# Gated projection in tall pieces: 1024 rows by 128 columns instead of 512 by 256

## The chip, the cores and the metric

The kernel runs on one core of a Trainium2 chip. The metric is the device time of one execution in microseconds. Before the change it is 2535.25 us, the median of three runs (2534.98 to 2535.69).

## The reference, cut to what matters

A decoder trunk of two layers over 256 positions of width 2048. Layer 0 mixes with gated DeltaNet heads and RG-LRU channels, layer 1 with sliding-window attention; each layer then cross-attends and applies a gated MLP. The change touches only the first product of layer 0, the combined input projection:

```python
h = rmsnorm(x, norm_mix[l])
if l % 2 == 0:
    qkv, z, b_raw, a_raw, lx, lg = split_cols(h @ hyb_in_w[e], HYB_SIZES)
    oa = gdn_mixer(qkv, z, b_raw, a_raw, ...)      # conv of width 4 and silu on q, k, v; chunked delta rule; gate z
    ob = rglru_mixer(lx, lg, ...)                  # conv of width 4, recurrence, gate lg
```

All is float32. `h @ hyb_in_w` is 256 x 2048 by 2048 x 6160 columns, of which the 16 for the gates are computed apart.

## The kernel before, in words

**Products in two parts.** Weights stream from HBM in pieces of 128x1024 values (512 KB), each as NK = 4 blocks of 128 rows by COLS = 256 columns. ScalarE rounds a piece to the matmul format (`w_hi`, L581), VectorE takes the rest (`w_lo`, L1048). The activations `h` are held as hi and low parts as well, side by side: `h[:, kt, 0]` and `h[:, kt, 1]`, 256 positions each. A product is hi x hi + hi x low + low x hi, three matmuls of 256 columns (L1754 to L1756). A group is 256 output columns: four pieces, 16 blocks of rows. Its result is one PSUM bank of 128 x 512: the two tiles of 128 channels, 256 positions each. Groups alternate between the banks ST[0] and ST[1]. A "wide" piece (L1759 to L1773), used elsewhere in the kernel, streams both parts of `h` in one matmul of 512 columns into two banks and leaves two halves that are added later.

**Order.** The hybrid stage has four pairs of heads, p = 0 to 3, each of 24 ticks, t = 0 to 23. One tick is one piece; six groups a pair, j = 0 to 5: q, k, v, z, the LRU's input, the LRU's gate (gi = 6p + j). On each engine the order is written out by hand. TensorE runs piece t (it waits for `lo_split` of that piece, and at the group's first piece for `group_evac` of the group two before), then the small products of `hyb_front(p, t)` for this pair and `hyb_tail(p - 1, t)` for the one before. ScalarE and VectorE run the split for piece t + 3 (AHEAD = 3) and then their own parts of front and tail; at t = 10 and 14 VectorE runs its front ahead of the split.

**Evacuation.** VectorE multiplies a finished bank by `rstd` (evac_scaled, L1053 to L1058): at t = 3, 7, 15, 19 and 23 right after the group's last piece, and for v (j = 2) only at t = 13, behind four mask products (L1266 to L1269) that wait for TensorE's products of tick 13 (`lx_done`). Destinations are the conv pads for q, k, v and the LRU input, `z_silu` for z and `k_buf` (as `gl_`) for the gate. The convs follow (L1100, L1103, L1111), then silu on ScalarE. Other steps that the prediction names: the squares and logs of q and k on ScalarE (L697 to L705), VectorE's output of the pair before (L1363, L1364), q and k normed (L1253, L1254), TensorE's grams (L1885), the mask products of levels (L1286), TensorE's chunk products (L1877, L1899), v_new (L1338), its use (L1982 to L1990), the state update (L1225), the scans (L1354), the LRU's decay (L1318).

**Loads.** SyncE issues a load (L447) as soon as `lo_split` has freed the raw buffer, four buffers in turn.

Of the kernel before, what the change touches and what calls it, by code (L numbers as in the profile page):

```python
# [26 lines left out]
ALU = mybir.AluOpType  # L27
# [3 lines left out]
P = 128  # L31
TOK = 256
# [21 lines left out]
COLS = 256  # L54
NRAW = 4
NSPLIT = 4
# [39 lines left out]
N_MEM = [0, 4]  # L96
N_XQ = [2, 16]
N_ROPE = 6


def mix_order(layer, t):
# [79 lines left out]
def trunk(nc, a, out):  # L181
    ctx = ExitStack()
    with ctx:
        def sb(name, shape, dt=F32, scope=ctx):
            return scope.enter_context(nc.sbuf_tensor(name, shape, dt))
# [50 lines left out]
        with s1:  # L236
            pads = sb("conv_pads", [P, 2, 2, TOK + 3], scope=s1)
            qb = sb("q_buf", [P, 512], scope=s1)
            kb = sb("k_buf", [P, 512], scope=s1)
            vbuf = sb("v_buf", [P, 512], scope=s1)  # L240
            zs = sb("z_silu", [P, 512], scope=s1)
            W4 = sb("gdn_work", [P, 4, 512], scope=s1)
            kbe = sb("k_beta_exp", [P, 512], scope=s1)
            kdec = sb("k_dec", [P, 512], scope=s1)
            vb = sb("v_beta", [P, 512], scope=s1)
            LT = sb("LT", [P, 512], scope=s1)
            Ufull = sb("U_blocks", [P, 512], scope=s1)
            qd = sb("q_dec", [P, 512], scope=s1)
            usb = sb("u", [P, 512], scope=s1)
            wsb = sb("wT", [P, 512], scope=s1)  # L250
            vnew = sb("v_new", [P, P], scope=s1)
            St = sb("state", [P, 256], scope=s1)
            egl = sb("exp_gl", [P, 8], scope=s1)
            ro = sb("o_rstd", [P, 512], scope=s1)
            xc = sb("lru_x", [P, 512], scope=s1)
            rt = sb("lru_r", [P, 512], scope=s1)
            it = sb("lru_i", [P, 512], scope=s1)
            l2 = sb("lru_l2", [P, 512], scope=s1)

            l1, gl_, osq = vbuf[:], kb[:], usb[:]  # L260
            msq = [qb[:], W4[:, 3, :]]
            ba_rows = usb[0:16, 0:TOK]
            x_ss, x_total, x_log, x_err = lp[:, 0, 0:8], lp[:, 1, 0:2], lp[:, 1, 2:4], lp[:, 1, 4:6]
# [81 lines left out]
        w_loaded = [sem(f"w_loaded{i}") for i in range(NRAW)]  # L345
        hi_split, lo_split = sem("hi_split"), sem("lo_split")
        pieces_done, group_evac = sem("pieces_done"), sem("group_evac")
        dve_link, act_link = sem("dve_link"), sem("act_link")
        x_loaded = [sem(f"x_loaded{i}") for i in range(4)]
        ident_loaded, c_loaded, p_loaded, b_loaded = sem("ident_loaded"), sem("c_loaded"), sem("p_loaded"), sem("b_loaded")  # L350
# [87 lines left out]
        @block.sync  # L438
        def _(sp):
            xv_ = a["x"].rearrange("b (t p) d -> p (b t) d", p=P)  # L440
            sp.dma_start(cst[:, 0:2 * P], a["consts"][:, 0:2 * P]).then_inc(ident_loaded, 16)

            def load(n, k, turn, src, rows, c0):

                if not isinstance(n, int) or n >= NRAW:
                    sp.wait_ge(lo_split, n - NRAW + 1)
                sp.dma_start(raw[:, k], src[rows:rows + NK * P, bass.ds(c0, COLS)]  # L447
                             .rearrange("(k p) c -> p k c", p=P)).then_inc(w_loaded[k], 16)

            def load_group(n, src, c0, quarters=4):  # L450
                for q in range(quarters):
                    if n == HYB:
                        sp.dma_start(x_tok[:, :, 512 * q:512 * q + 512], xv_[:, :, 512 * q:512 * q + 512]).then_inc(x_loaded[q], 16)
                    load(n + q, (n + q) % NRAW, 0, src, q * NK * P, c0)
                if n == HYB:
                    sp.dma_start(cst[:, 2 * P:], a["consts"][:, 2 * P:]).then_inc(c_loaded, 16)

            hyb = a["hyb_in_w"][0]
            starts = [0, 1024, 2048, 3072, 4112, 5136]
            for p in range(PAIRS):  # L460
                for j, s in enumerate(starts):
                    load_group(HYB + p * PAIR_TICKS + 4 * j, hyb, s + p * COLS)

            def load_mem(layer):
                for g in range(4):
                    load_group(MEM[layer] + 4 * g, a["xkv_w"][layer], g * COLS)

            def load_common(layer, mixout):
                for t in range(32):
                    g, q = mix_order(layer, t)  # L470
                    load(MIXOUT[layer] + t, t % NRAW, 0, mixout, q * NK * P, g * COLS)
                for g in range(2):
                    load_group(XQ[layer] + 4 * g, a["xq_w"][layer], g * COLS)
                if layer == 0:
                    load_mem(1)
                for g in range(8):
                    load(XO[layer] + g, g % NRAW, 0, a["xo_w"][layer], 0, g * COLS)
                for c, size, tile, n, g in ffn_parts(layer):
                    with sp.Fori(0, size // 2) as i:
                        for half in range(2):  # L480
                            for q in range(4):
                                load(n + 4 * half + q + i * 8, q, 0, a["ffn_in_w"][layer], q * NK * P,
                                     half * F_FF + tile * P + i * COLS)
                    n += 4 * size
                    quarters = size // 4
                    for g in range(8):
                        for q in range(quarters):
                            load(n + g * quarters + q, (g * quarters + q) % NRAW, 0, a["ffn_out_w"][layer],
                                 (tile + 4 * q) * P, g * COLS)

            load_mem(0)
            load_common(0, a["hyb_out_w"][0])
            for g in range(4):
                load_group(SWKV + 4 * g, a["swa_in_w"][0], SWA_HEADS * SWA_HD + g * COLS)
            for g in range(8):
                load_group(SWQ + 4 * g, a["swa_in_w"][0], g * COLS)
            load_common(1, a["swa_out_w"][0])
            for s in o_stored:
                sp.wait_ge(s, 16 * 4)
# [538 lines left out]
        def _(dve):  # L1038
# [14 lines left out]
            def evac_scaled(dst, start, gi, n, i=0, rows=rstd):  # L1053
# [3 lines left out]
                bank = B[4] if gi in (GROUP[XQ[0]], GROUP[SWKV]) else ST[gi % 2]  # L1057
                v.tensor_tensor(dst, two(bank[:]), r, ALU.mult).then_inc(group_evac, 1)  # L1058

            def refine(r, u, total, width):  # L1060

                link(v.scalar_tensor_tensor(u, total, EPS * width, r, ALU.add, ALU.mult))
                link(v.scalar_tensor_tensor(u, u, -0.5 / width, r, ALU.mult, ALU.mult))
                return v.scalar_tensor_tensor(r, u, 1.5, r, ALU.add, ALU.mult)
# [164 lines left out]
            def hyb_front(p, t):  # L1229
# [40 lines left out]
                if t in (3, 7, 13):  # L1270
                    if t == 13:
                        j, gi, n = 2, gi - 1, n - 2
                    if p:
                        if j < 2:
                            dve.wait_ge(lt_ready, p)
                        else:
                            dve.wait_ge(vT_done, p)
                    evac_scaled(pads[:, gi % 2, :, 3:3 + TOK], HYB, gi, n)
                    dve.wait_ge(group_evac, gi + 1)
                    if t == 3 and p:  # L1280
                        state_update(p - 1, 3)
                    qkv_conv(p, j, (0,) if t == 13 else (0, 1))
# [6 lines left out]
                if t == 19:  # L1289
                    if p:  # L1290
                        dve.wait_ge(lru_out, p)
                    evac_scaled(pads[:, gi % 2, :, 3:3 + TOK], HYB, gi, n)
                if t >= 15 and t % 2:
                    dve.wait_ge(tu_done, 5 * p + level)
                    dve.wait_ge(tu_ready, 6 * p + level)
# [8 lines left out]
                if t == 15:  # L1304
                    if p:
                        dve.wait_ge(gdn_out, p)
                    evac_scaled(two(zs[:]), HYB, gi, n)
                if t == 19:
                    pad = pads[:, gi % 2]
                    dve.wait_ge(group_evac, gi + 1)  # L1310
# [7 lines left out]
                        last = v.tensor_scalar(rt[:, s], rt[:, s], 1.0, lruc[:, 2, 2 * p + b:2 * p + b + 1], ALU.add, ALU.mult)  # L1318
                    last.then_inc(la_ready, 1)
                if t == 23:  # L1320
                    evac_scaled(two(gl_), HYB, gi, n)

            def hyb_tail(p, t):
                if t == 0:
# [56 lines left out]
            for p in range(PAIRS):  # L1381
                for t in range(PAIR_TICKS):
# [16 lines left out]
                    if p:  # L1399
                        hyb_tail(p - 1, t)  # L1400
                    elif t not in (6, 10, 11):
                        gates(t)
                    if p == 1 and t == 0:
                        kq = lambda name: par[:, PCOL[name]:PCOL[name] + DEPTH]
                        link(v.tensor_tensor(key_gain, kq("xq_norm"), kq("xk_norm"), ALU.mult))
# [323 lines left out]
        def _(pe):  # L1729
# [8 lines left out]
            def piece(n, gi, q, last_q, src, kts, bank=None, between=None):  # L1738
# [17 lines left out]
                        last = mm(o, wlo[:, k, kk, w], src[:, kt, 0, :], start=False, stop=final, skip_group_check=True)  # L1756
                last.then_inc(pieces_done, 1)

            def wide_piece(n, gi, q, kts, i, src=h, last_q=3):  # L1759

                k = n % NSPLIT
# [268 lines left out]
            for p in range(PAIRS):  # L2030
                for t in range(PAIR_TICKS):
                    if p == 0 and t < 4:
                        h_is("x")(t)
                    piece(HYB + PAIR_TICKS * p + t, 6 * p + t // 4, t % 4, 3, h, range(4 * (t % 4), 4 * (t % 4) + 4))
                    hyb_front(p, t)
                    if p:
                        hyb_tail(p - 1, t)
# [368 lines left out]
```

## Time and profile before

| | |
|---|---|
| median of three runs | 2535.25 us |
| profiled execution | 2536.81 us |
| its span | 2535.0 us |
| granted TensorE clock | 0.999 |
| TensorE, VectorE, ScalarE busy | 99%, 69%, 45% |
| hybrid stage | pieces 0 to 95, up to about 409 us |

The times in the rows further down are microseconds from the start of the span. A matmul's length in a row includes its way through the array, so rows of consecutive matmuls overlap: the distance of their starts is what one costs.

### The profile page before, as it was taken

How to read it: one execution, taken by the hardware profiler on the slowest of the kernel's cores; microseconds unless marked ns; L12 is line 12 of the kernel's file. 1: busy time of each engine (PE TensorE's matmuls, PEld its weight loads, DVE VectorE, ACT ScalarE, POOL GpSimd, SP SyncE). 2: the span in 40 equal slices, each digit the busy share in tenths (PEclk: the TensorE clock that was granted, in tenths of full speed). 3: DMA queues.
4: the chain of work that ended last, by engine and by line, in shares of the span. 5: the costliest groups of instructions: out<-in, count | busy, mean ns of one | idle time of the engine just before them, and what ended most of it. 6: DMA issues, size and time to landing. Idle time of an engine off the chain costs nothing.

```text
span 2535.0 us, 44491 instructions
## 1 busy us (share of the span) xinstructions
PE 2510.7 (99%) x17345; PEld 2257.2 (89%) x17345; DVE 1757.0 (69%) x2483; ACT 1143.6 (45%) x1532; POOL 50.1 (2%) x58
## 2 busy tenths in 40 slices
PE   8999999999999999999999999999999999999999
PEld 7999998989988888888888999998888888888888
DVE  6676676677777657775678767776777667765774
ACT  6444455445444434443444445544444334433443
POOL 2000000010000000000000000010000000000000
PEclk9999999999999999999999999999999999999999
DMA  7444444554565655665565543353555655655654
GB/s 221 126 142 125 134 133 135 180 188 157 158 190 183 193 188 178 195 193 188 183 191 182 177 138 114 125 175 125 172 179 187 199 188 184 192 191 176 197 191 149
DMA packets 428439, 432.34 MB, mean 171 GB/s; under 512 B 13802, under 2 KB 425747, under 8 KB 428304
## 3 DMA queue, kind: packets, MB, share of 16 engines
q1 hardware_dynamic: 423776, 422.46, 52.9%
q0 software_dynamic: 2304, 5.85, 0.8%
q8 instruction: 99, 1.62, 0.3%
q10 hardware_dynamic: 2224, 2.11, 0.3%
q14 instruction: 36, 0.29, 0.0%
HBM read 428.27 MB, written 2.10 MB: 170 GB/s over the span
## 4 chain that ended last, share of the span: by engine, by line
PE 94%; DVE 3%; ACT 2%; issue 1%; DMA 0%; SPq 0%; ACTq 0%; DVEq 0%
PE stream L1769 41%; PE stream L1772 20%; PE stream L1754 8%; PE stream L1755 8%; PE stream L1756 8%; PE bank L1877 1%; PE bank L1736 1%; DVE w_lo L1048 1%; ACT w_hi L581 1%; DVE k_buf L1111 0%; PE bank L2322 0%; PE bank L1945 0%; PE bank L1804 0%; PE bank L2296 0%; PE bank L2303 0%
## 5 line engine op out<-in xcount | busy, mean ns | idle before, releaser
L1048 DVE TENSOR_TENSOR w_lo<-w_raw,w_hi 128x1024 fp32r<-128x1024 f32 x800 | 963.3, 1222 | 476.7 <-ACT w_hi L581 473.9
L581 ACT CAST w_hi<-w_raw 128x1024 fp32r<-128x1024 f32 x800 | 835.9, 1049 | 748.9 <-PE stream L1772 628.7
L1769 PE MATMUL stream<-h,w_hi 128*128 128x512 f32 x2816 | 884.7, 395 | 0.0
L1772 PEld LDWEIGHTS stream<-h,w_lo 128*128 128x128 f32 x2816 | 529.0, 188 | 125.1
L1772 PE MATMUL stream<-h,w_lo 128*128 128x256 f32 x2816 | 553.2, 278 | 0.0
L1769 PE MATMUL stream<-act,w_hi 128*128 128x512 f32 x1664 | 523.3, 396 | 0.0
L1754 PE MATMUL stream<-h,w_hi 128*128 128x256 f32 x1536 | 455.2, 296 | 2.2 <-DVE w_lo L1048 2.2
L1755 PE MATMUL stream<-h,w_hi 128*128 128x256 f32 x1536 | 435.2, 283 | 0.0
L1756 PE MATMUL stream<-h,w_lo 128*128 128x256 f32 x1536 | 435.1, 283 | 0.0
L1769 PEld LDWEIGHTS stream<-h,w_hi 128*128 128x128 f32 x2816 | 428.8, 189 | 0.1
L1772 PEld LDWEIGHTS stream<-act,w_lo 128*128 128x128 f32 x1664 | 312.6, 188 | 73.9
L1772 PE MATMUL stream<-act,w_lo 128*128 128x256 f32 x1664 | 327.0, 278 | 0.0
L1754 PEld LDWEIGHTS stream<-h,w_hi 128*128 128x128 f32 x1536 | 294.6, 192 | 16.3 <-issue 11.3
L1755 PEld LDWEIGHTS stream<-h,w_hi 128*128 128x128 f32 x1536 | 295.0, 192 | 4.0 <-issue 3.6
L1756 PEld LDWEIGHTS stream<-h,w_lo 128*128 128x128 f32 x1536 | 294.8, 192 | 0.0
L1769 PEld LDWEIGHTS stream<-act,w_hi 128*128 128x128 f32 x1664 | 253.4, 189 | 0.0
L1482 DVE TENSOR_TENSOR ffn_cross<-stream,ffn_cross 128x512 f32<-128x512 f32 x88 | 60.9, 692 | 96.3 <-ACT ffn_cross L930 96.3
L930 ACT COPY ffn_cross<-stream 128x512 f32<-128x512 f32 x88 | 51.7, 587 | 152.5 <-PE stream L1772 152.5
L1754 PE MATMUL stream<-act,w_hi 128*128 128x256 f32 x336 | 97.8, 291 | 0.0
L1755 PE MATMUL stream<-act,w_hi 128*128 128x256 f32 x336 | 95.1, 283 | 0.0
L1756 PE MATMUL stream<-act,w_lo 128*128 128x256 f32 x336 | 95.1, 283 | 0.0
L1111 DVE SCALAR_TENSOR_TENSOR ffn_conv<-ffn_pad,par,ffn_conv 128x256 f32<-128x256 f32 x176 | 77.5, 482 | 13.1 <-DVE ffn_conv L1103 6.7
(425 smaller groups left out, 1887.9 us busy)
## 6 DMA issues: line engine op xcount, KB each, us to landing
w_raw<-in_ffn_in_w SPq DMA_DIRECT2D x352, 512.0 KB, 4.4
w_raw<-in_ffn_out_w SPq DMA_DIRECT2D x176, 512.0 KB, 3.4
w_raw<-in_hyb_in_w SPq DMA_DIRECT2D x96, 512.0 KB, 3.8
w_raw<-in_swa_in_w SPq DMA_DIRECT2D x48, 512.0 KB, 3.5
w_raw<-in_xkv_w SPq DMA_DIRECT2D x32, 512.0 KB, 3.4
w_raw<-in_hyb_out_w SPq DMA_DIRECT2D x32, 512.0 KB, 4.4
w_raw<-in_swa_out_w SPq DMA_DIRECT2D x32, 512.0 KB, 3.6
w_raw<-in_xq_w SPq DMA_DIRECT2D x16, 512.0 KB, 4.1
```

Source lines behind the costliest of these rows:

```text
L581: nc.scalar.copy(whi[:, k], raw[:, n % NRAW]).then_inc(hi_split, 1)
L930: nc.scalar.copy(two(frt[:, t // 4]), wide(g0 + t // 4)[:, :, TOK:512]).then_inc(ffn_right, 1)
L1048: v.tensor_tensor(wlo[:, k], raw[:, n % NRAW], whi[:, k].bitcast(F32), ALU.subtract).then_inc(lo_split, 1)
L1111: last = v.scalar_tensor_tensor(d, tap, par[:, col(j, b)], d, ALU.mult, ALU.add)
L1482: v.tensor_tensor(two(frt[:, t // 4]), both[:, :, 0:TOK], two(frt[:, t // 4]), ALU.add).then_inc(group_evac, 1)
L1736: return nc.tensor.transpose(o, i, ident)
L1754: mm(o, whi[:, k, kk, w], src[:, kt, 0, :], start=first, stop=False, skip_group_check=True)
L1755: mm(o, whi[:, k, kk, w], src[:, kt, 1, :], start=False, stop=False, skip_group_check=True)
L1756: last = mm(o, wlo[:, k, kk, w], src[:, kt, 0, :], start=False, stop=final, skip_group_check=True)
L1769: mm(bank[:, m, :], whi[:, k, kk, w], src[:, kt, :, :], start=(q == 0 and kk == 0), stop=False, skip_group_check=True)
L1772: last = mm(bank[:, m, 0:TOK], wlo[:, k, kk, w], src[:, kt, 0, :], start=False, stop=(q == last_q and kk == len(kts) - 1), skip_group_chec ...
L1877: last = mm(bank[rows, o + u * CHUNK:o + u * CHUNK + CHUNK], lhs[rows, s], rhs[rows, s], start=True, stop=True)
```

## The change

For 22 of the 24 groups (all but the first and the last) a piece has another shape: 1024 rows by 128 columns. A group's pieces 0 and 1 are then the first tile of 128 channels over all 2048 rows, and pieces 2 and 3 the second tile. The raw, hi and low buffers are the same memory, read as 8 blocks of 128 rows and 128 columns. Each block is one matmul of 512 columns (hi weights with hi and low parts of `h`) and one of 256 (low weights with the hi part), into one bank per tile: the first tile has ST[1], the second ST[0]. VectorE multiplies the bank by `rstd` into `tile_parts` and adds its two halves into the destination. The first tile is evacuated at the end of VectorE's ticks t = 2, 6, 10, 14, 18, 22, the second where the whole group was. TensorE waits at a group's first piece for `first_tile_evac` of the group before, and at its third for `group_evac` of the group before.

```diff
+TALL = range(1, 6 * PAIRS - 1)
+def tall(slot):
+    return slot.rearrange("p a (b c) -> p (a b) c", c=P)
...
+            def load_tall(n, src, c0):
+                for i in range(4):
+                    m, half = i // 2, i % 2
+                    if n + i >= NRAW:
+                        sp.wait_ge(lo_split, n + i - NRAW + 1)
+                    sp.dma_start(tall(raw[:, (n + i) % NRAW]),
+                                 src[half * 8 * P:half * 8 * P + 8 * P, c0 + m * P:c0 + m * P + P]
+                                 .rearrange("(k p) c -> p k c", p=P)).then_inc(w_loaded[(n + i) % NRAW], 16)
...
+            def evac_tile(dst, gi, m, n):
+                dve.wait_ge(pieces_done, n + 1)
+                dve.wait_ge(first_tile_evac if m else group_evac, gi)
+                bank = ST[1 - m]
+                link(v.tensor_tensor(two(parts[:]), two(bank), rstd[:].unsqueeze(1).to_broadcast([P, 2, TOK]), ALU.mult))
+                v.tensor_tensor(dst, parts[:, 0:TOK], parts[:, TOK:512], ALU.add).then_inc(group_evac if m else first_tile_evac, 1)
+            def evac_hyb(p, j, n, tiles):
+                gi = 6 * p + j
+                pad = pads[:, gi % 2]
+                for m in tiles:
+                    flat = slice(m * TOK, m * TOK + TOK)
+                    evac_tile(zs[:, flat] if j == 3 else gl_[:, flat] if j == 5 else pad[:, m, 3:3 + TOK], gi, m, n)
...
-                    evac_scaled(pads[:, gi % 2, :, 3:3 + TOK], HYB, gi, n)
+                    if gi in TALL:
+                        evac_hyb(p, j, n, (1,))
+                    else:
+                        evac_scaled(pads[:, gi % 2, :, 3:3 + TOK], HYB, gi, n)
...
+                    if t % 4 == 2 and 6 * p + t // 4 in TALL:
+                        if t == 14 and p:
+                            dve.wait_ge(gdn_out, p)
+                        evac_hyb(p, t // 4, HYB + PAIR_TICKS * p + t - 1, (0,))
...
+            def tall_piece(n, gi, t):
+                k, m, half = n % NSPLIT, t // 2, t % 2
+                pe.wait_ge(lo_split, n + 1)
+                if half == 0 and m == 0 and gi > 1:
+                    pe.wait_ge(first_tile_evac, gi - 1)
+                if half == 0 and m == 1:
+                    pe.wait_ge(group_evac, gi)
+                bank, hi, lo = ST[1 - m], tall(whi[:, k]), tall(wlo[:, k])
+                for kk in range(0, 8, 2):
+                    for e in (kk, kk + 1):
+                        mm(bank, hi[:, e, :], h[:, 8 * half + e, :, :], start=(half == 0 and e == 0), stop=False, skip_group_check=True)
+                    for e in (kk, kk + 1):
+                        last = mm(bank[:, 0:TOK], lo[:, e, :], h[:, 8 * half + e, 0, :], start=False,
+                                  stop=(half == 1 and e == 7), skip_group_check=True)
+                last.then_inc(pieces_done, 1)
...
-                    piece(HYB + PAIR_TICKS * p + t, 6 * p + t // 4, t % 4, 3, h, range(4 * (t % 4), 4 * (t % 4) + 4))
+                    if 6 * p + t // 4 in TALL:
+                        tall_piece(HYB + PAIR_TICKS * p + t, 6 * p + t // 4, t % 4)
+                    else:
+                        if 6 * p + t // 4 == TALL[-1] + 1 and t % 4 == 0:
+                            pe.wait_ge(first_tile_evac, len(TALL))
+                        piece(HYB + PAIR_TICKS * p + t, 6 * p + t // 4, t % 4, 3, h, range(4 * (t % 4), 4 * (t % 4) + 4))
```

The evacuations at t = 15, 19 and 23 change in the same way as the one shown.

## Rows read from the trace of the kernel before

**Rows 1.** The page: busy time by engine, and the chain by engine.
```profile
PE 2510.7 (99%) x17345; PEld 2257.2 (89%) x17345; DVE 1757.0 (69%) x2483; ACT 1143.6 (45%) x1532; POOL 50.1 (2%) x58
...
PE 94%; DVE 3%; ACT 2%; issue 1%; DMA 0%; SPq 0%; ACTq 0%; DVEq 0%
```

**Rows 2.** Timeline of TensorE, old pieces in pair 0 (start us, length us, ...).
```profile
43.16 0.28 PE L1756 MATMUL stream<-h,w_lo 128*128 128x256 f32 x1
...
49.28 0.28 PE L1756 MATMUL stream<-h,w_lo 128*128 128x256 f32 x1
```

**Rows 3.** Timeline of TensorE, wide pieces of the FFN.
```profile
1000.25 0.39 PE L1772 MATMUL stream<-h,w_lo 128*128 128x256 f32 x2
...
1011.39 0.39 PE L1772 MATMUL stream<-h,w_lo 128*128 128x256 f32 x2
```

**Rows 4.** Timeline of TensorE and VectorE, pair 1, tick 13 and piece 14.
```profile
169.90 0.68 PE L1899 MATMUL bank<-cst,LT 64*64 64x64 f32 x16 [0.22 <-DVE q_dec L1262]
...
170.52 0.39 PE L1754 MATMUL stream<-h,w_hi 128*128 128x256 f32 x1
...
170.90 0.42 DVE L1266 TENSOR_TENSOR gdn_work<-bank,cst 128x256 f32<-128x256 f32 x1
...
172.03 0.42 DVE L1269 TENSOR_TENSOR gdn_work<-cst,gdn_work 128x256 f32<-128x256 f32 x1
...
172.37 0.68 DVE L1058 TENSOR_TENSOR conv_pads<-stream,rstd 128x512 f32<-128x512 f32 x1
```

**Rows 5.** Timeline of VectorE, pair 1, tick 14, and TensorE's piece 16.
```profile
175.03 0.42 DVE L1286 TENSOR_TENSOR gdn_work<-bank,cst 128x256 f32<-128x256 f32 x1
...
177.19 1.22 DVE L1048 TENSOR_TENSOR w_lo<-w_raw,w_hi 128x1024 fp32r<-128x1024 f32 x1
...
178.33 0.39 PE L1754 MATMUL stream<-h,w_hi 128*128 128x256 f32 x1
```

**Rows 6.** Timeline of VectorE, pair 2, ticks 2 to 4; TensorE's piece 4 and tick 5.
```profile
225.22 1.27 DVE L1354 TENSOR_TENSOR_SCAN lru_x<-lru_r,lru_i 128x256 f32<-128x256 f32 x2
226.53 1.23 DVE L1048 TENSOR_TENSOR w_lo<-w_raw,w_hi 128x1024 fp32r<-128x1024 f32 x1
...
233.33 0.28 DVE L1338 TENSOR_TENSOR v_new<-u,bank 128x128 f32<-128x128 f32 x1
...
227.17 0.39 PE L1754 MATMUL stream<-h,w_hi 128*128 128x256 f32 x1
...
233.67 0.66 PE L1990 MATMUL stream<-q_dec,state 128*128 128x64 f32 x4
```

**Rows 7.** Timeline of VectorE, pair 1, ticks 7 to 10; TensorE's grams of tick 11.
```profile
144.99 0.69 DVE L1058 TENSOR_TENSOR conv_pads<-stream,rstd 128x512 f32<-128x512 f32 x1 [1.14 <-PE stream L1756]
...
159.29 0.69 DVE L1254 TENSOR_TENSOR k_buf<-k_buf,gdn_work 128x512 f32<-128x512 f32 x1
...
160.03 0.45 PE L1885 MATMUL bank<-k_buf 128*64 128x64 f32 x8
```

**Rows 8.** Timeline of VectorE, pair 0, ticks 6 and 7.
```profile
46.71 2.36 DVE L1048 TENSOR_TENSOR w_lo<-w_raw,w_hi 128x1024 fp32r<-128x1024 f32 x2
49.24 0.69 DVE L1058 TENSOR_TENSOR conv_pads<-stream,rstd 128x512 f32<-128x512 f32 x1 [0.17 <-PE stream L1756]
```

**Rows 9.** Timeline of VectorE, pair 1, tick 22, and TensorE's next piece 0.
```profile
209.52 0.61 DVE L1318 TENSOR_SCALAR lru_r<-lru_r,lru_cols 128x256 f32<-128x256 f32 x2
...
211.28 0.39 PE L1754 MATMUL stream<-h,w_hi 128*128 128x256 f32 x1
```

**Rows 10.** Busy time from 100 to 410 us (window, us, engines, clock, DMA, GB/s).
```profile
100.00:410.00 310.00, 307.72 (x3128) 287.16 (x3127) 214.32 (x362) 154.46 (x225) 1.42 (x2) 1.00 0.44 131
```

**Rows 11.** The casts (page), queue 1 from 200:300, the gain queue from 0:8.
```profile
L581 ACT CAST w_hi<-w_raw 128x1024 fp32r<-128x1024 f32 x800 | 835.9, 1049 | 748.9 <-PE stream L1772 628.7
...
q1 hardware_dynamic: 13276, 13.19, 45.0%
...
q10 hardware_dynamic: 48, 0.02, 0.8%
```

More of the change, by code:

```diff
@@ L239, in trunk @@
             kb = sb("k_buf", [P, 512], scope=s1)
+            parts = sb("tile_parts", [P, 512], scope=s1)
             vbuf = sb("v_buf", [P, 512], scope=s1)
@@ L347, in trunk @@
         pieces_done, group_evac = sem("pieces_done"), sem("group_evac")
+        first_tile_evac = sem("first_tile_evac")
         dve_link, act_link = sem("dve_link"), sem("act_link")
@@ L461, in _ @@
                 for j, s in enumerate(starts):
-                    load_group(HYB + p * PAIR_TICKS + 4 * j, hyb, s + p * COLS)
+                    if 6 * p + j in TALL:
+                        load_tall(HYB + p * PAIR_TICKS + 4 * j, hyb, s + p * COLS)
+                    else:
+                        load_group(HYB + p * PAIR_TICKS + 4 * j, hyb, s + p * COLS)
             def load_mem(layer):
@@ L1291, in hyb_front @@
                         dve.wait_ge(lru_out, p)
-                    evac_scaled(pads[:, gi % 2, :, 3:3 + TOK], HYB, gi, n)
+                    evac_hyb(p, j, n, (1,))
                 if t >= 15 and t % 2:
@@ L1306, in hyb_front @@
                         dve.wait_ge(gdn_out, p)
-                    evac_scaled(two(zs[:]), HYB, gi, n)
+                    evac_hyb(p, j, n, (1,))
                 if t == 19:
@@ L1320, in hyb_front @@
                 if t == 23:
-                    evac_scaled(two(gl_), HYB, gi, n)
+                    if gi in TALL:
+                        evac_hyb(p, j, n, (1,))
+                    else:
+                        evac_scaled(two(gl_), HYB, gi, n)
             def hyb_tail(p, t):
@@ L2033, in _ @@
                         h_is("x")(t)
-                    piece(HYB + PAIR_TICKS * p + t, 6 * p + t // 4, t % 4, 3, h, range(4 * (t % 4), 4 * (t % 4) + 4))
+                    if 6 * p + t // 4 in TALL:
+                        tall_piece(HYB + PAIR_TICKS * p + t, 6 * p + t // 4, t % 4)
+                    else:
+                        if 6 * p + t // 4 == TALL[-1] + 1 and t % 4 == 0:
+                            pe.wait_ge(first_tile_evac, len(TALL))
+                        piece(HYB + PAIR_TICKS * p + t, 6 * p + t // 4, t % 4, 3, h, range(4 * (t % 4), 4 * (t % 4) + 4))
                     hyb_front(p, t)
```

## The prediction

> **What bounds the kernel now.** I read the page first: TensorE is busy 99% of the span and makes 94% of the chain of waits, VectorE is busy 69% [rows 1]. So every microsecond that TensorE waits is a microsecond of the run, and VectorE costs nothing until something on TensorE waits for it. Then I read the timeline of the hybrid stage engine by engine, because the change moves the points at which TensorE may wait for VectorE. I write "piece t" and "tick t" for tick t of a pair, 0 to 23; TensorE's small products of a tick stand behind its piece. TensorE waits in this stage only a few tenths at a time (0.22 us for the end of LT's group, [rows 4]), and what VectorE does in a tick is late by design: its split at tick t is for the piece of tick t+3.
>
> **The piece itself.** The old piece has 24 matmuls of 256 columns. From 43.16 to 49.28 us lie 51 of them [rows 2]: 0.120 each, 2.88 us a piece. The tall piece has 8 of 512 and 8 of 256, in the order of the wide piece that layer 0 and the FFN run: two 512, two 256. Sixteen such fours take 1011.39 - 1000.25 = 11.14 us [rows 3], 0.696 each, four to a piece: 2.785 us. Saved: 0.095 us a piece, 88 pieces, 8.4 us if nothing else moves. The columns streamed are the same (6144); only the eight fewer instructions are saved. No row shows two 512s into one bank; the old pieces' 256s all go to one bank and hold 0.120, so I bound that from 0 to 8.4 us for all and take 0.095 a piece. The Trainium skill (TensorE: Matmul & The Clock Gate, "Back-to-back issue gap") gives an isolated matmul N/2.4 + 2.5 ns, which would be 109 and 216 ns, a saving of 0.02 us a piece; the rows have 120 and a mean of 174, so the trace pays more per instruction than that rule, and by the rule the sum below would be some 2.4 us higher.
>
> **What VectorE gets.** Per group one multiply of 128x512 (0.69 [rows 4]) becomes two, each followed by a linked add of 128x256, which I price with the 0.42 of the 128x256 product of the same engine [rows 4]: 0.69 + 0.04 for the link + 0.42 = 1.15 us a tile, 2.3 a group, some 1.6 x 22 = 35 us more work. VectorE has the room on average [rows 10]. Not everywhere: the bank turns round faster. Before, a group had its bank for two groups' time; the evacuation at tick 4j+3 was needed at piece 4j+8. Now tile 1 of group j, still evacuated there, is needed by piece 4j+6, and tile 0, evacuated at the very end of VectorE's tick 4j+2, by piece 4j+4. I laid these needs over the timeline in all four pairs; the rows repeat in each to a few hundredths.
>
> **(e) Tick 13, the large one.** Group j=2 is evacuated not at tick 11 but at tick 13, behind four mask products that wait for TensorE's products of tick 13. TensorE starts piece 14 at 170.52, right behind those. VectorE starts the masks at 170.90 and the evacuation only at 172.37 [rows 4]. Piece 14 is now the first of tile 1 and waits for exactly that evacuation: 172.37 + 0.69 + 0.04 + 0.42 + 0.05 to cross = 173.57. Stall 3.05 us, in each pair: 12.2 us. It can't be hidden: the masks need TensorE's tick 13, which stands directly ahead of piece 14. Queued behind it on TensorE is everything.
>
> **(g) Tick 14.** After the evacuation VectorE has half a conv, a mask, the other half and a split, and only then tile 0 of j=3, which piece 16 needs. Before, from the mask at 175.03 to the split at 177.19 are 2.16 us, and piece 16 starts at 178.33 [rows 5]. With TensorE's products of tick 14 now ending near 177.3, mask 177.3, split 179.4 to 180.7, tile 0 until 181.7; TensorE could start piece 16 at 181.2. +0.5 us a pair.
>
> **(b) Ticks 2 to 5, pairs 1 to 3.** Tick 2 ends with two scans, and the split of tick 3 starts at 226.53; piece 4 starts at 227.17 [rows 6]. Tile 0 of j=0 goes between, with 0.3 us of delay from gelu and ScalarE's queue (the added 0.46 on the evacuation of tick 23): scans end 226.7, tile 0 227.9, piece 4 at 227.95: +0.8. Then the row of VectorE work from the split at 226.53 to v_new at 233.33 has no gap, and TensorE's product at 233.67 wants v_new, which is done at 233.61 [rows 6]. That row starts 1.3 us later and has 0.46 more in it: v_new at 235.4, the product at 235.4, +1.75 in all. By tick 7 VectorE has caught up.
>
> **(d) Ticks 7 to 11.** From the end of piece 7 there is one closed chain: evacuation 144.99, conv, silu, squares, a table load, the log and exp of o, VectorE's output of the pair before, the norm of k at 159.29, TensorE's grams at 160.03 [rows 7]. The add lengthens it by 0.46. Pieces 8 to 11 end earlier, for nothing. In pair 0 that chain has other parts: the split at 46.71 and its follower run without a gap up to the evacuation at 49.24 [rows 8], tile 0 of j=1 goes between, and conv and the gate values behind it come 1.4 later; TensorE has some 0.2 there to give, so +1.2.
>
> **(a) Piece 0 of the next pair.** The scale of lru_r ends at 210.13, tile 0 of j=5 follows until 211.3, piece 0 starts at 211.28 [rows 9]: +0.07, and the savings of pieces 22 and 23 go into it, since the chain before it runs over ScalarE.
>
> **What of the saving remains.** Where a chain over VectorE decides, shorter pieces wait. It remains for pieces 6, 7, 14 and 16 to 21 (nine in pairs 1 and 2, seven in pairs 0 and 3): 32 of 88, 3.0 us. The others had it taken by (a), (b), (d), (g) and by the chain over exp and LT before tick 13, where TensorE already waited [rows 4].
>
> **The loads.** Each row of a load is 512 bytes instead of 1024, 1024 packets instead of 512. Between 200 and 300 us queue 1 used 45.0% of 16 x 100 us for 13276 packets, 54 ns each with the tiny ones; the gain load's queue had 0.8% of 16 x 8 us for 48 packets, 32 of them of 512 bytes: at most 32 ns each [rows 11]. So a load needs 64 x 32 = 2.0 us of each DMA engine against 1.7, in a tick of 4.07 us on average (piece 16 at 178.33, piece 4 of the next pair at 227.17, twelve ticks [rows 5, 6]). ScalarE's casts wait for TensorE, not for a load [rows 11]. I take 0; bounds 0 and, were packets as dear as before (3.5 us in a tick of 4.07), some 5. The Trainium skill (DMA: Bandwidth & Descriptors, "Why small descriptors are slow") has a fixed three cycles a packet on 32-byte beats: 2 x 19 / 35, 9% more DMA time, nothing for the run either; the rows allow 17% and more.
>
> **Sum.** (e) 4 x 3.05 = 12.2. (g) 4 x 0.5 = 2.0. (b) 3 x 1.75 = 5.25, in which the saving of its pieces is already spent. (d) 3 x 0.46 + 1.2 = 2.6. (a) 3 x 0.07 = 0.2. Less 3.0. Together +19.2 us. The profiled execution took 2536.81 us (span 2535.0, 1.8 around it), so 2556.0 for it; it lies 1.6 above the median 2535.25, so 2554.5 for a median. Behind the hybrid stage TensorE is again at work without a break, so nothing of it is given back.
>
> **Rivals.**
> 1. Only the wait at piece 14 is real, the smaller ones lie within slack that I misjudge (the add is shorter, TensorE's waits take up what VectorE is late). For it: my margins in (a), (b), (g) are tenths. Against: the row of VectorE work in (b) has no gap at all. 12.2 less the saving of 80 pieces, 7.6: +4.6, 2540.
> 2. Faster: the wait isn't there, because group j=2's bank is free by piece 14, and all pieces keep their 0.095. It decides at one point: the evacuation at 172.37 would have to end before 170.5. Against it: that evacuation stands behind work that itself waits for TensorE. 2535.25 - 8.4 = 2526.9.
> 3. The lateness of VectorE feeds on itself: splits come late, ScalarE (silu, casts) behind them, and piece 6, 10 or 18 waits too. For it: VectorE is busy 214 of 310 us in the stage [rows 10], 69%, and the 35 us more make it 80%. Against it: the split that ends at 178.41 is for piece 17, which can't start before piece 16 at 178.33 has run its 2.88 [rows 5], so splits have some 3 us to give. Another 2.5 us a pair: +29, 2564.
> 4. Loads become late: another 5 on the sum, 2559.5; it needs packets as dear as double the size.
>
> **Chances.** Forecast 0.62, rival 1 0.14, rival 2 0.04, rival 3 0.14, rival 4 0.03; the rest (0.03) is that 512-column matmuls into one bank go slower. A measurement of this kernel tells 0.2% (5 us) from no change. Faster 0.04, same 0.07 (half of rival 1), slower 0.89. The range of 8 in 10 is 2543 to 2564: below it lie rival 2 and most of rival 1, above it part of rival 3.
>
> **What would show it.** (e): TensorE idle by about 3 us before one tall matmul in each pair, released by VectorE's add into conv_pads. (b): a wait of 0.8 for the add at piece 4 and about 1 for v_new. (g): 0.5 before piece 16. Piece: 0.696 per four. Loads: landing of hyb_in under 5 us, no cast that waits for one. I am wrong if piece 14 starts without a wait, or if the hybrid stage is longer by under 10 or over 28 us, or if the rest of the run changes.

## The result, and the profile after

The changed kernel takes 2564.26 us (2563.52 to 2564.79, four runs) against 2535.47 beside it: ratio 1.0114, 95% interval 1.0102 to 1.0125, 28.8 us slower. Forecast were 19.2 us and a range of 2543 to 2564. The direction and the waits held; the sum was a third short, mainly because one term was missing from it, the price of a halved clock behind each long wait, and the time lies 0.26 us outside the range.

The two profiled executions are 28.0 us apart (2564.79 and 2536.81). Piece 96, the first behind the hybrid stage, starts at 440.42 us against 412.25, 28.2 later; from there to the end both take the same (2122.6 and 2122.7 us). The prediction's own sign of being wrong, a stage longer by over 28, was thus met.

The page after, with busy time by engine, the chain by engine, and the groups of the tall piece (L1818, L1820), the old piece (L1802) and the split (L1070):

```profile
PE 2513.1 (98%) x16641; PEld 2225.4 (87%) x16641; DVE 1787.6 (70%) x2549; ACT 1143.4 (45%) x1532; POOL 50.1 (2%) x58
...
PE 88%; DVE 7%; ACT 3%; issue 2%; DMA 0%; DVEq 0%; SPq 0%; ACTq 0%
...
L1818 PE MATMUL stream<-h,w_hi 128*128 128x512 f32 x704 | 236.2, 417 | 18.0 <-DVE conv_pads L1088 15.0
L1802 PE MATMUL stream<-h,w_hi 128*128 128x256 f32 x832 | 246.1, 296 | 1.7 <-DVE w_lo L1070 1.7
L1820 PE MATMUL stream<-h,w_lo 128*128 128x256 f32 x704 | 142.1, 284 | 0.0
```

Beside [rows 1], TensorE has fallen from 94% of the chain to 88% and VectorE has risen from 3% to 7%: the chain now runs through VectorE where TensorE waits. Of the 18.0 us that TensorE sat idle before the tall matmuls of L1818, 15.0 were ended by the add into conv_pads.

The timeline of TensorE in pair 1, from the products of tick 13 to piece 15, answers to [rows 4] (start, length, then the idle time before and what ended it):

```profile
178.32 0.68 PE L1964 MATMUL bank<-cst,LT 64*64 64x64 f32 x16 [0.38 <-DVE q_dec L1300]
182.06 0.76 PE L1818 MATMUL stream<-h,w_hi 128*128 128x512 f32 x2 [3.06 <-DVE conv_pads L1088]
182.61 0.63 PE L1820 MATMUL stream<-h,w_lo 128*128 128x256 f32 x2
183.04 1.05 PE L1818 MATMUL stream<-h,w_hi 128*128 128x512 f32 x2
183.90 0.63 PE L1820 MATMUL stream<-h,w_lo 128*128 128x256 f32 x2
184.33 1.05 PE L1818 MATMUL stream<-h,w_hi 128*128 128x512 f32 x2
185.18 0.63 PE L1820 MATMUL stream<-h,w_lo 128*128 128x256 f32 x2
185.61 0.80 PE L1818 MATMUL stream<-h,w_hi 128*128 128x512 f32 x2
```

The wait for the add is there with 3.06 us, as forecast. What I had not forecast stands in the rows behind it: a four of matmuls (two of 512 columns, two of 256) takes 1.29 us (183.04 to 184.33) instead of 0.70. The same stretches by the windows view (window, its length, busy PE, PEld, DVE, ACT, POOL, granted clock, DMA share, GB/s):

```profile
76.60:83.40 6.80, 5.89 (x26) 4.92 (x28) 2.54 (x6) 0.00 (x0) 0.00 (x0) 0.51 0.23 68
83.40:182.40 99.00, 92.08 (x768) 77.42 (x766) 74.82 (x130) 47.56 (x68) 0.00 (x0) 1.00 0.49 128
182.50:185.90 3.40, 3.40 (x13) 2.96 (x12) 1.29 (x3) 0.00 (x0) 0.00 (x0) 0.51 0.05 13
186.00:284.80 98.80, 92.55 (x774) 77.74 (x772) 73.86 (x126) 47.57 (x68) 0.00 (x0) 1.00 0.48 125
284.90:288.30 3.40, 2.85 (x9) 2.51 (x10) 2.21 (x5) 0.00 (x0) 0.00 (x0) 0.51 0.36 107
288.40:387.20 98.80, 93.33 (x778) 78.39 (x777) 73.10 (x125) 47.57 (x68) 0.00 (x0) 1.00 0.47 123
387.40:394.10 6.70, 5.55 (x19) 4.60 (x20) 2.77 (x6) 0.00 (x0) 0.00 (x0) 0.50 0.22 75
```

In each pair, about when the wait at piece 14 ends, the granted clock falls to half (1.2 instead of 2.4 GHz), for 6.8, 3.4, 3.4 and 6.8 us, and is whole again until the next. Before the change it was 1.00 in all of this stage. The Trainium skill (TensorE: Matmul & The Clock Gate, "What's actually happening") says that the array's clock is gated to half when the engine has been idle and given back by activity; these rows agree in kind, each fall standing behind 3.06 or 3.07 us of idle time, and I had left that rule out of the sum.

### The profile page after: what moved, and what is told of

Its sections match the earlier page's. It is cut to its first block, busy times and chain, and to the rows that moved or that the text cites. A ratio compares the mean times of both kernels' runs of the same rounds, so it can differ in the third digit from the quotient of the medians.

```text
span 2563.0 us, 43197 instructions
## 1 busy us (share of the span) xinstructions
PE 2513.1 (98%) x16641; PEld 2225.4 (87%) x16641; DVE 1787.6 (70%) x2549; ACT 1143.4 (45%) x1532; POOL 50.1 (2%) x58
## 4 chain that ended last, share of the span: by engine, by line
PE 88%; DVE 7%; ACT 3%; issue 2%; DMA 0%; DVEq 0%; SPq 0%; ACTq 0%
PE stream L1834 41%; PE stream L1837 20%; PE stream L1802 5%; PE stream L1803 5%; PE stream L1804 5%; PE stream L1818 3%; DVE w_lo L1070 2%; PE stream L1820 1%; PE bank L1784 1%; ACT w_hi L603 1%; PE bank L1942 1%; DVE tile_parts L1087 1%; ACT L609 1%; DVE k_buf L1149 0%; DVE q_buf L1149 0%
## 5 line engine op out<-in xcount | busy, mean ns | idle before, releaser
L1070 DVE TENSOR_TENSOR w_lo<-w_raw,w_hi 128x1024 fp32r<-128x1024 f32 x800 | 963.6, 1221 | 469.0 <-ACT w_hi L603 466.4
L1834 PE MATMUL stream<-h,w_hi 128*128 128x512 f32 x2816 | 884.8, 396 | 0.0
L1837 PE MATMUL stream<-h,w_lo 128*128 128x256 f32 x2816 | 553.1, 278 | 0.0
L1834 PEld LDWEIGHTS stream<-h,w_hi 128*128 128x128 f32 x2816 | 428.8, 189 | 0.1
L1837 PE MATMUL stream<-act,w_lo 128*128 128x256 f32 x1664 | 327.0, 278 | 0.0
L1818 PE MATMUL stream<-h,w_hi 128*128 128x512 f32 x704 | 236.2, 417 | 18.0 <-DVE conv_pads L1088 15.0
L1802 PE MATMUL stream<-h,w_hi 128*128 128x256 f32 x832 | 246.1, 296 | 1.7 <-DVE w_lo L1070 1.7
L1803 PE MATMUL stream<-h,w_hi 128*128 128x256 f32 x832 | 236.0, 284 | 0.0
L1804 PE MATMUL stream<-h,w_lo 128*128 128x256 f32 x832 | 235.9, 284 | 0.0
L1802 PEld LDWEIGHTS stream<-h,w_hi 128*128 128x128 f32 x832 | 159.8, 192 | 9.0 <-issue 8.3
L1820 PEld LDWEIGHTS stream<-h,w_lo 128*128 128x128 f32 x704 | 135.8, 193 | 32.5
L1803 PEld LDWEIGHTS stream<-h,w_hi 128*128 128x128 f32 x832 | 160.0, 192 | 2.4 <-issue 2.2
L1820 PE MATMUL stream<-h,w_lo 128*128 128x256 f32 x704 | 142.1, 284 | 0.0
L1818 PEld LDWEIGHTS stream<-h,w_hi 128*128 128x128 f32 x704 | 111.2, 194 | 27.1 <-issue 23.7
```

Source lines behind the costliest of these rows:

```text
L1070: v.tensor_tensor(wlo[:, k], raw[:, n % NRAW], whi[:, k].bitcast(F32), ALU.subtract).then_inc(lo_split, 1)
L1802: mm(o, whi[:, k, kk, w], src[:, kt, 0, :], start=first, stop=False, skip_group_check=True)
L1803: mm(o, whi[:, k, kk, w], src[:, kt, 1, :], start=False, stop=False, skip_group_check=True)
L1818: mm(bank, hi[:, e, :], h[:, 8 * half + e, :, :], start=(half == 0 and e == 0), stop=False, skip_group_check=True)
L1820: last = mm(bank[:, 0:TOK], lo[:, e, :], h[:, 8 * half + e, 0, :], start=False, stop=(half == 1 and e == 7), skip_group_check=True)
L1834: mm(bank[:, m, :], whi[:, k, kk, w], src[:, kt, :, :], start=(q == 0 and kk == 0), stop=False, skip_group_check=True)
```

## The experiments

Each was timed in three or five rounds beside the kernel before (2535.2 to 2535.6). The "step" at piece t is by how much the time from the start of piece t to that of piece t + 1 is longer than in the kernel that it is compared with. Steps come from the one profiled execution of each kernel. The expectations set theory A (the wait leaves TensorE idle, the clock falls behind that, and both cost time) against B (the tall pieces lower the clock, whatever the wait) and C (the slow pieces have nothing to do with the clock).

**early_v.** One line of the change is undone in its effect: v's second tile is evacuated where VectorE had been idle.

```diff
                     last.then_inc(dmin, 1)                 # tick 11
+                    evac_hyb(p, 2, n, (1,))
...                                                         # and no longer at tick 13
```

> The changed kernel, with the second tile of v (j = 2) evacuated at the end of VectorE's front of tick 11, where VectorE was idle for 1.9 us, instead of behind the masks of tick 13. Theory A (the wait of 3.1 to 3.2 us at piece 14 costs itself and lets the granted clock fall behind it, which costs another 1.3 to 2.7 a pair, 8 us in all): the wait and the four falls of the clock both go, the conv of v comes 1.1 us earlier so that most of the 0.6 before piece 16 goes too; 2564.3 - 12.8 - 8 - 2 = 2541 to 2543, granted clock 0.999. Theory B (the clock falls because of the tall pieces themselves, whatever the wait): only the wait goes, the clock stays at 0.995, 2549 to 2551. Theory C (the slow pieces 14 and 15 are a wait of another kind): as B in time, with the clock either way.

Measured: 2545.46 us (2543.65 to 2546.45), ratio 1.0039 (1.0024 to 1.0053), granted clock 0.999 in all five executions. VectorE, pair 1, ticks 11 to 13, and the clock of the stage (1.00, last but two):

```profile
166.70 0.86 DVE L1278 TENSOR_SCALAR gdn_work<-stream,small 128x64 f32<-128x64 f32 x4 [0.49 <-PE stream L1988]
167.47 0.68 DVE L1087 TENSOR_TENSOR tile_parts<-stream,rstd 128x512 f32<-128x512 f32 x1
168.19 0.43 DVE L1088 TENSOR_TENSOR conv_pads<-tile_parts 128x256 f32<-128x256 f32 x1
169.53 1.22 DVE L1070 TENSOR_TENSOR w_lo<-w_raw,w_hi 128x1024 fp32r<-128x1024 f32 x1 [0.91 <-ACT w_hi L603]
...
60.00:420.00 360.00, 345.34 (x2969) 292.52 (x2968) 274.08 (x480) 174.12 (x261) 1.43 (x2) 1.00 0.50 131
```

The pair of L1087 and L1088 fits into the idle time ahead of the split, of which 0.91 us is left, and piece 14 starts without a wait. One moved evacuation gives back 18.8 of 28.8 us. The time lies between what A and B had given; the clock, whole at every piece 14, speaks for A. It is 2.5 above A's 2543, mainly because the wait before piece 16 stayed (0.63, 0.99, 0.63, 0.63): its chain starts with TensorE's products of tick 14, not with v's evacuation.

**filler.** The wait stays, its idle time goes.

```diff
                 if half == 0 and m == 1:
+                    if gi % 6 == 3:
+                        for _ in range(13):
+                            mm(B[3][:], hi[:, 0, :], h[:, 0, :, :], start=True, stop=True, skip_group_check=True)
                     pe.wait_ge(group_evac, gi)
```

> The changed kernel; ahead of the wait at piece 14 TensorE runs 13 matmuls of 512 columns into the bank of T and U, which nothing reads before it is written anew (2.8 us of work in the place of the idle time, so the wait for the evacuation ends when it did). Theory A: the time of the wait stays, the clock doesn't fall: 2564.3 - 8 = 2556, granted clock 0.999, piece 14 takes 2.8 us again. Theory B (tall pieces lower the clock) and theory C (not the clock): 2564 still, B with 0.995.

Measured: 2555.65 us (2554.58 to 2558.18), ratio 1.0083 (1.0066 to 1.0099), granted clock 0.999 in all four executions against 0.995 to 0.996. TensorE, pair 1, and the windows around piece 14 of the four pairs:

```profile
175.84 3.24 PE L1817 MATMUL bank<-h,w_hi 128*128 128x512 f32 x13
178.92 0.69 PE L1821 MATMUL stream<-h,w_hi 128*128 128x512 f32 x2
179.45 0.40 PE L1823 MATMUL stream<-h,w_lo 128*128 128x256 f32 x2
179.69 0.62 PE L1821 MATMUL stream<-h,w_hi 128*128 128x512 f32 x2
```
```profile
69.90:90.00 20.10, 19.03 (x165) 15.94 (x164) 15.89 (x29) 8.94 (x17) 0.00 (x0) 1.00 0.42 107
172.00:190.00 18.00, 16.93 (x141) 14.14 (x140) 15.67 (x28) 6.84 (x13) 0.00 (x0) 1.00 0.38 95
273.00:292.00 19.00, 17.99 (x149) 14.95 (x147) 15.64 (x28) 7.90 (x15) 0.00 (x0) 1.00 0.41 104
375.00:395.00 20.00, 19.00 (x165) 15.86 (x164) 15.65 (x28) 8.90 (x17) 0.00 (x0) 1.00 0.41 112
```

Piece 14 still starts 3.08 us (178.92 - 175.84) after TensorE could have started it, but with the clock at 1.00. The kernel is 8.6 us faster for doing 52 useless matmuls. The steps at piece 14 are shorter by 2.73, 1.56, 1.35 and 2.54 us than in the changed kernel, 8.2 together: that is the price of the clock, and B and C fall, since tall pieces and wait are both still there.

**filler_half.** Six of the matmuls instead of thirteen.

> The changed kernel with 6 instead of 13 filling matmuls at piece 14: of 3.1 us some 1.8 stay idle. Theory A1 (a fall takes nearly all of the idle time): none, 2556 as with 13. Theory A2 (1.8 us idle are enough in some pairs): one to four falls, 2558 to 2564.

Measured: 2554.81 us (2553.46 to 2555.95), ratio 1.0076 (1.0060 to 1.0093). TensorE, pair 1:

```profile
177.13 1.65 PE L1817 MATMUL bank<-h,w_hi 128*128 128x512 f32 x6
180.18 0.73 PE L1821 MATMUL stream<-h,w_hi 128*128 128x512 f32 x2 [1.39 <-DVE conv_pads L1088]
...
60.00:420.00 360.00, 341.39 (x2902) 287.77 (x2901) 267.08 (x468) 166.75 (x246) 0.72 (x1) 1.00 0.48 125
```

Some 1.4 us stay idle by the row, not the 1.8 that I had expected, and the clock did not fall in any pair (1.00 in the stage; steps at piece 14 shorter by 2.70, 1.52, 1.31, 2.50). That fits A1 for 1.4 us and leaves 1.8 untested.

**wait_only.** The kernel before with one wait that its data doesn't need, so that neither the tall pieces, nor the loads, nor the adds are there.

```diff
+                if n < MEM[0] and n % PAIR_TICKS == 14:
+                    pe.wait_ge(group_evac, gi)
```

> The kernel before, with old pieces, loads and evacuations; only the wait is added: piece 14 of each pair waits for v's evacuation. Nothing of its data needs it. By the rows of before the evacuation of 172.37 ends at 173.05, so TensorE waits 2.6 us a pair, 10.4 in all. Theory A: the clock falls behind the wait as in the changed kernel, perhaps not in all pairs as the wait is 0.5 shorter: 2535.4 + 10.4 + 4 to 8 = 2550 to 2554, clock 0.996. Theory B: clock 0.999, 2546. If VectorE's chain takes the wait up later in the pair: below 2546.

Measured: 2552.26 us (2550.07 to 2553.97), ratio 1.0066 (1.0049 to 1.0083), clock 0.996 to 0.998. The step at piece 13 is 2.68 in all four pairs, 10.7 us, and piece 14 then takes another 1.47, 2.53, 1.31 and 1.44. The execution with the clock at 0.998 is the shortest of the four (2550.07). The wait in pair 1, and two of its windows:

```profile
176.59 0.55 PE L1756 MATMUL stream<-h,w_hi 128*128 128x256 f32 x1 [2.61 <-DVE conv_pads L1058]
...
76.60:80.00 3.40, 3.40 (x19) 3.40 (x18) 0.97 (x2) 0.00 (x0) 0.00 (x0) 0.50 0.04 14
175.70:182.40 6.70, 5.81 (x32) 5.62 (x34) 2.55 (x6) 0.00 (x0) 0.00 (x0) 0.50 0.26 76
```

So this single wait brings 17 us into a kernel without any of the change's other parts, and theory B falls here too.

**wait_filled.** The same wait, with eleven matmuls ahead of it.

> The kernel before with the added wait at piece 14, and 11 matmuls of 512 columns ahead of it that fill 2.35 of its 2.7 us (into the bank of T and U, read by nothing). Theory A: the wait's own 2.7 us a pair stay, the clock doesn't fall: 2535.5 + 10.7 = 2546, against 2552.3 with the wait left idle; granted clock 0.999. Theory B (the fall has nothing to do with idle time): 2552.

Measured: 2545.86 us (2544.93 to 2547.19), ratio 1.0041 (1.0026 to 1.0055), clock 0.999 to 1.000. The windows view of the stage:

```profile
60.00:420.00 360.00, 358.17 (x3653) 333.51 (x3652) 242.35 (x411) 173.64 (x259) 1.42 (x2) 1.00 0.44 130
```

It is 10.6 us above the kernel before, four steps of 2.62 to 2.64 at piece 13; the other 6.4 of wait_only were the clock.

**release.** TensorE waits for the multiply that reads the bank, not for the add behind it.

```diff
-                link(v.tensor_tensor(two(parts[:]), two(bank), ..., ALU.mult))
+                v.tensor_tensor(two(parts[:]), two(bank), ..., ALU.mult).then_inc(bank_free[m], 1)
+                dve.wait_ge(bank_free[m], gi)
...
-                    pe.wait_ge(first_tile_evac, gi - 1)
+                    pe.wait_ge(bank_free[0], gi - 1)
...
-                    pe.wait_ge(group_evac, gi)
+                    pe.wait_ge(*((bank_free[1], gi - 1) if gi > 1 else (group_evac, 1)))
```

> The changed kernel, but TensorE waits for the multiply alone, which is what frees the bank, and not for the add behind it. Theory A: every wait for an evacuation is 0.46 us shorter: at piece 14 four times, at piece 16 four times, at piece 4 three times, at pieces 0 and 8 the few tenths that there are; about 5 us, 2559, with the clock falling as before. What the adds put into VectorE's chains (v_new, the norm of k) stays. Rival D (the add is hidden, another event lets TensorE go): 2564.

Measured: 2560.33 us (2559.03 to 2561.22), ratio 1.0099 (1.0083 to 1.0116). The steps before pieces 14 and 16 are 0.45 to 0.47 shorter in each pair, as expected. Before piece 4 they are too, but all of that comes back: 0.24 to 0.26 at piece 4 and 0.20 to 0.23 at piece 5, at v_new, which the adds delay as before. Its clock fell five times, at piece 14 of each pair (behind 2.61 us of idle time) and once more at 56.5 us behind a wait of 1.99 us in tick 9 of pair 0, for 3.4 us each. So the gain of 3.9 us is not that of the shorter waits alone: the falls at pieces 14 cost 2.1 less, the new one some 1.7 more.

**all_early.** All 22 groups stay tall; VectorE's order is made for it. It has the edits of early_v and release as well.

```diff
+                    if t == 22 and 6 * p + 5 in TALL:              # ahead of the split
+                        evac_hyb(p, 5, HYB + PAIR_TICKS * p + 21, (0,))
...
+                    if t == 2 and p < PAIRS - 1:                   # behind v_new, ahead of the LRU
+                        evac_hyb(p + 1, 0, HYB + PAIR_TICKS * (p + 1) + 1, (0,))
...                                                                 # state_update first in tick 3; q's second half in tick 4
```

> All 22 groups tall as in the changed kernel, but VectorE's order made for it: v's second tile at tick 11, TensorE released by the multiply, the first tile of j = 3 ahead of v's second conv half, that of j = 5 ahead of the split of tick 22, that of j = 0 ahead of the LRU's work of tick 2, the state update ahead of the evacuation of tick 3 and q's second conv half behind v_new. Theory A (what is left of the loss is VectorE's work where it has no idle time, ticks 1 to 10: 3.0 us more between 221 and 246 us, where it had 1.9 idle): no wait at pieces 4 and 16, none for v_new, but the grams of tick 11 come 1 to 1.4 later than before; 2536 to 2540, granted clock 0.999. Theory E (only the places of the waits cost, not the amount of VectorE's work): every wait goes and the savings of 88 pieces remain but for the chain before tick 13, 2530.

Measured: 2544.66 us (2543.93 to 2545.95), ratio 1.0036 (1.0022 to 1.0050). Neither theory's number. The waits at pieces 4 and 16 went, but others took their place. TensorE in pair 0, tick 9, and pair 2, tick 6:

```profile
55.91 1.55 PE L1987 MATMUL bank<-gdn_work,cst 128*128 128x512 f32 x2 [1.98 <-ACT gdn_work L724]
...
243.32 0.44 PE L2045 MATMUL bank<-state,wT 128*64 128x128 f32 x4 [1.00 <-DVE state L1268]
```

The first is followed by a fall of the clock at 56.4 us; the step there is 3.20. The second is in pairs 1 to 3 (0.98, 0.99, 0.98), the state update of tick 5 now late; at piece 17 there is 0.53 in each pair. At pieces 2 and 5 steps of 0.34 to 0.48 stay, and 0.45 at the grams of tick 11. The loss thus lies largely in VectorE's ticks 1 to 10, as A says, but the kernel is 9.1 us above the one before where I had at most 5; whether the amount of work makes it or the new order, this run doesn't separate. How low a better order could come with all groups tall stays open.

**late_tall** and **two_groups.** The tall groups only where VectorE has idle time, with the first tile in ST[0] and the second in ST[1].

```diff
-TALL = range(1, 6 * PAIRS - 1)
+TALL = [g for g in range(6 * PAIRS - 2) if g % 6 >= 2]     # late_tall; two_groups: >= 4
...
-                bank, hi, lo = ST[1 - m], tall(whi[:, k]), tall(wlo[:, k])
+                bank, hi, lo = ST[m], tall(whi[:, k]), tall(wlo[:, k])
```

> Tall pieces only for groups j = 2 to 5 (14 groups, without the last two), where VectorE has idle time; q and k are as before. The order as in the run above; the first tile has ST[0], the second ST[1], so that the normal groups between fit without a wait. Theory A: pieces 14 to 23 of three pairs and 14 and 15 of the last keep 0.07 to 0.09 each, the others lose theirs to chains; 32 x 0.08 = 2.5 us less than before, 2533, no new wait over 0.2. Were even these absorbed: 2535.4.

> Tall pieces only for j = 4 and 5 of the first three pairs (6 groups, 24 pieces), v evacuated at tick 13 as before. Theory A: 24 x 0.08 = 1.9 us less than before, 2533.5. If the first tile of j = 5 in tick 22 or the longer evacuations of ticks 19 and 23 (0.46 each) are in the way: 2535 to 2536.

Measured: late_tall 2535.84 us, ratio 1.0000 (0.9991 to 1.0009); two_groups 2534.37 us, ratio 0.9995 (0.9986 to 1.0004), beside 2535.59. late_tall was expected at 2533; it loses its saving again at piece 17 (0.5 a pair), in tick 11 (0.25) and at piece 2 (0.2). two_groups' trace has the stage shorter by 1.64 us at piece 96, but that is only by luck near the 1.9 expected: its 24 tall pieces save 1.7, pieces 2 and 5 of the next pairs lose 0.9 of it, and 0.9 come from a wait for a load that before's profiled execution has and two_groups' has not:

```profile
405.12 1.09 PE L1736 MATMUL bank<-cst,stage 128*128 128x128 f32 x8 [0.70 <-DMA stage<-in_mem]
```

wait_filled and filler_half don't have that wait either, after has one of 1.21 us: it belongs to the execution and not to the tall pieces. two_groups' median is 1.2 us lower, but the interval holds no change: it isn't shown to beat the kernel before.

## Why the prediction was wrong, step by step

- **(e) Tick 13:** right. 3.06 us idle for the add; the steps at piece 13 are 3.20 us in each pair against 3.05, 12.8 against 12.2.
- **The missing term, the step that failed:** the sum took the wait of (e) at 4 x 3.05, its own length, and let piece 14 keep its saving. The clock behind the wait stood at nothing. Steps at piece 14 are 2.62, 1.45, 1.23 and 2.43 us where I had -0.09: 8.1 us in all, and 8.2 by filler. With these steps 19.2 becomes 27.3. To the stage's 28.2, (e) and (g) took 0.6 us each more than booked, and smaller terms of either sign make up the rest. Nothing in the rows of before warned of it in this stage, where the clock was whole and no wait came near 3 us. But the same trace has one fall behind the stage, which I passed over (TensorE, at the products of x_probs):

```profile
1752.87 0.66 PE L1736 MATMUL stream<-cst,x_probs 128*128 128x128 f32 x4 [1.21 <-DVE x_probs L1450]
1754.46 1.12 PE L1736 MATMUL bank<-cst,x_probs 128*128 128x128 f32 x4 [0.93 <-DVE x_probs L1450]
...
1754.30:1757.70 3.40, 3.24 (x15) 3.24 (x16) 0.10 (x1) 1.53 (x2) 0.00 (x0) 0.50 0.00 0
```

  A rival "after each long wait the clock falls" should have stood there with a price.
- **(g) Tick 14:** right in kind, 0.63 to 0.70 a pair against 0.5. Its row:

```profile
192.03 0.70 PE L1818 MATMUL stream<-h,w_hi 128*128 128x512 f32 x2 [0.72 <-DVE z_silu L1088]
```

- **(b) Ticks 2 to 5:** right. These rows answer to [rows 6]; from piece 0 to piece 6 each pair lost 1.65 us against 1.75:

```profile
241.24 0.70 PE L1818 MATMUL stream<-h,w_hi 128*128 128x512 f32 x2 [0.77 <-DVE conv_pads L1088]
...
248.59 0.55 PE L2055 MATMUL stream<-q_dec,state 128*128 128x64 f32 x3 [0.98 <-DVE v_new L1382]
```

- **(d) Ticks 7 to 11:** from piece 7 to piece 12 +0.37 a pair against 0.46, and +1.47 in pair 0 against 1.2. **(a)** 0.12 against 0.07.
- **The piece:** fours in a row take 0.696 (41.02, 41.71, 42.41), the price of [rows 3], here with both 512s into one bank. But pieces with small products around them gained 0.07, not 0.095: 32 of them some 0.8 us less than booked.

```profile
41.02 0.63 PE L1818 MATMUL stream<-h,w_hi 128*128 128x512 f32 x2
...
41.71 0.63 PE L1818 MATMUL stream<-h,w_hi 128*128 128x512 f32 x2
...
42.41 0.63 PE L1818 MATMUL stream<-h,w_hi 128*128 128x512 f32 x2
```

- **The loads:** right, nothing. Queue 1 from 200 to 300 us after the change, against [rows 11]:

```profile
q1 hardware_dynamic: 24382, 12.29, 47.1%
...
w_raw<-in_hyb_in_w SPq DMA_DIRECT2D x22, 512.0 KB, 3.9
```

Twice the packets at 31 ns each with the tiny ones (47.1% of 1600 us by 24382), and a landing of 3.9 us.

- **The rivals:** the time came out at that of rival 3 (2564), but not by its mechanism: in pairs 1 to 3 no wait of TensorE for a split is in the trace. Rival 3 also set the upper end of the range, so that the range was missed by so little is luck. Rivals 1, 2 and 4 fall.

## What to carry to other kernels

A change that turns a buffer round twice as fast has to be laid against the order of the engine that empties it; here the largest wait could be read off to a tenth of a microsecond (3.05 against 3.06), the smaller ones to two tenths. A wait of about 3 us on a TensorE that was hardly ever idle costs more than its length: here 1.3 to 2.7 us on top for the halved clock behind it. Filling it with matmuls that nobody reads gave back that part (8.2 us of 8.1); moving the evacuation gave back the wait as well.

## What was not expected of the hardware

The clock fell behind idle times of 2.6 us (wait_only, release) and 3.1 us (after) in every pair, twice behind 2.0 us (all_early, release, tick 9 of pair 0), and not behind 1.4 us (filler_half, four times) nor 1.5 us (after and early_v, tick 9 of pair 0). Lengths between 1.5 and 2.6 us were not tried by themselves.

The length of the wait doesn't decide alone. The fall behind the stage, with waits of 1.21 and 0.93 us ahead of it, is in six of the eleven profiled executions (before, after, early_v, filler, wait_filled, all_early), and not in the other five, which have the same waits at the same place. From piece 96 to the end the six take 2122.5 to 2123.0 us and the five 2121.0 to 2121.3, so this one fall costs some 1.6 us and may be part of the scatter of all times here; the 1.6 us by which the prediction's profiled execution lay above its median has the same size. Why it comes in one execution and not in another stays open.

The price goes by how long the clock stays low: with 3.4 us of it the steps at piece 14 are 1.2 to 1.5 us, with 6.8 us they are 2.4 to 2.6. The same wait was followed by either.
